# First weights between the input halves, value fills after the second gate, stick-breaking scores inside attention, and an output projection begun on two tiles

## The reference

```python
h = rms_norm(x, norm1_w[l])
cols = split_cols(h @ w_in[l], IN_SIZES)
y_a = short_conv_mixer(a_b, a_c, a_u, conv_w[l], conv_b[l])
y_b = nsa_mixer(...)          # 4 heads: compressed, selected and windowed attention
y_c = mla_mixer(...)          # 4 heads, causal
y_d = stick_breaking_mixer(...)   # 4 heads
y = rms_norm(concat(y_a, y_b, y_c, y_d) in 4 groups of 256)
x = x + y @ w_out[l]
x = x + square(relu(rms_norm(x) @ ffn_w1[l])) @ ffn_w2[l]
```

```python
z = einsum('bqhd,bkhd->bhqk', q_blk, k) * scale
log_1m = where(strict, log_sigmoid(-z), 0.0)
rem = cumsum(log_1m, reverse=True) - log_1m
a = where(strict, exp(log_sigmoid(z) + rem), 0.0)
```

## Time and profile before

| what | value |
| --- | --- |
| time, median of 3 runs | 1802.92 us (1802.78 to 1804.18) |
| the profiled execution's own time | 1803.52 us |
| its span in the trace | 1801.4 us |
| PE busy | 1737.8 us (96% of the span), 8107 matmuls |
| DVE, ACT, POOL busy | 969.2, 692.2, 203.3 us (54%, 38%, 11%) |
| share of the chain that ended last | PE 89%, DVE 5%, ACT 2%, issue 2%, DMA 1% |

### The profile page before, as it was taken

One profiled execution on the slowest core, in us unless ns is written; L12 is line 12 of the kernel. 1 busy time (PEld: TensorE's weight loads), 2 busy tenths in 40 slices (PEclk: granted clock), 3 DMA queues, 4 the chain that ended last, 5 costly groups with the idle time before them and its releaser, 6 DMA issues.

```text
span 1801.4 us, 20984 instructions
## 1 busy us (share of the span) xinstructions
PE 1737.8 (96%) x8107; PEld 1376.0 (76%) x8107; DVE 969.2 (54%) x1724; ACT 692.2 (38%) x1243; POOL 203.3 (11%) x167
## 2 busy tenths in 40 slices
PE   7999999999999999999999899999999999999998
PEld 4557778566888888887788787775887888888887
DVE  4465476343563333346655788875444555556334
ACT  3233344552433233234464545552424422223234
POOL 3233100002100000012000233320200200000000
PEclk9999999899999999999999999999999999999999
DMA  6243201213433323233122011113330223332221
GB/s 186 80 132 95 94 24 48 76 59 99 126 94 94 102 94 108 95 94 98 55 70 71 12 59 59 48 59 99 123 106 1 94 94 97 106 101 94 94 94 47
DMA packets 122371, 152.23 MB, mean 85 GB/s; under 512 B 8827, under 2 KB 110609, under 8 KB 121762
## 3 DMA queue, kind: packets, MB, share of 16 engines
q1 hardware_dynamic: 119986, 140.19, 24.5%
q0 software_dynamic: 2288, 10.71, 1.7%
HBM read 144.90 MB, written 6.00 MB: 84 GB/s over the span
## 4 chain that ended last, share of the span: by engine, by line
PE 89%; DVE 5%; ACT 2%; issue 2%; DMA 1%; POOL 0%; DVEq 0%; ACTq 0%; POOLq 0%
PE bank L1953 50%; PE bank L1987 16%; PE bank L1261 2%; PE bank L1654 2%; PE bank L2198 2%; PE bank L2309 2%; PE bank L1212 1%; PE bank L2282 1%; PE bank L2195 1%; PE bank L774 1%; PE bank L1124 1%; PE bank L1129 1%; PE bank L1351 1%; PE bank L1687 1%; PE bank L2084 1%
## 5 line engine op out<-in xcount | busy, mean ns | idle before, releaser
L1953 PE MATMUL bank<-act_high,w_high 128*128 128x512 f32 x1360 | 553.0, 407 | 13.2 <-issue 4.6
L1953 PE MATMUL bank<-act_high,w_low 128*128 128x512 f32 x1360 | 533.1, 392 | 0.0
L1953 PE MATMUL bank<-act_low,w_high 128*128 128x512 f32 x1360 | 532.3, 391 | 0.0
L643 ACT ACTIVATE w_high<-ring 128x1024 fp32r<-128x1024 f32 x222 | 234.4, 1057 | 680.9 <-PE bank L1953 466.9
L667 DVE TENSOR_TENSOR w_low<-ring,w_high 128x1024 fp32r<-128x1024 f32 x202 | 254.7, 1262 | 221.9 <-ACT w_high L643 221.9
L1953 PEld LDWEIGHTS bank<-act_high,w_high 128*128 128x128 f32 x1360 | 257.6, 189 | 75.0 <-issue 16.8
L1953 PEld LDWEIGHTS bank<-act_high,w_low 128*128 128x128 f32 x1360 | 256.7, 189 | 55.2
L1953 PEld LDWEIGHTS bank<-act_low,w_high 128*128 128x128 f32 x1360 | 257.8, 190 | 51.8 <-issue 3.6
L1987 PE MATMUL bank<-act_high,w_high 128*128 128x512 f32 x416 | 162.2, 390 | 2.4 <-DVE arena L3192 1.2
L1987 PE MATMUL bank<-act_high,w_low 128*128 128x512 f32 x416 | 162.0, 389 | 0.0
L1987 PE MATMUL bank<-act_low,w_high 128*128 128x512 f32 x416 | 162.0, 389 | 0.0
(11 more groups left out here) (361 smaller groups left out, 2187.8 us busy)
## 6 DMA issues: line engine op xcount, KB each, us to landing
ring<-in_ffn_w SPq DMA_DIRECT2D x32, 1024.0 KB, 5.3
ring<-in_w_in SPq DMA_DIRECT2D x28, 1024.0 KB, 5.4
ring<-in_w_up SPq DMA_DIRECT2D x22, 1024.0 KB, 5.1
ring<-in_w_down SPq DMA_DIRECT2D x11, 1024.0 KB, 5.0
ring<-in_w_mem_kv SPq DMA_DIRECT2D x8, 1024.0 KB, 5.4
ring<-in_cmp_w SPq DMA_DIRECT2D x4, 1024.0 KB, 7.9
ring<-in_w_out SPq DMA_DIRECT2D x4, 1024.0 KB, 5.5
ring<-in_w_mix_out SPq DMA_DIRECT2D x4, 1024.0 KB, 5.3
```

What stands on the lines that cost most here:

```text
L643: nc.scalar.activation(part(w_high, name), raw_part(name), ACT.Copy).then_inc(w_rounded, 1)
L1953: last = nc.tensor.matmul(b[0:rows, :], w[:, k, 0:rows], a, start=k == 0 and n == 0, stop=k == KT - 1 and n == 2)
```

## The change

1. **Start.** SP fetches m_q between the halves of x. ACT rounds cq0 after two squares, and cq1 after two act_high. POOL splits both before it waits for x_in[1]. PE runs pieces of cq0 and cq1 between the turns and square sums of the second half. cq0 and cq1 get banks 4 and 5, all later tiles shift in their turn of banks.
2. **Value fills.** The three memsets go from DVE's work at 101 to 106 us to behind its second gate of the short convolution (`conv_gate(1)`, 166 us before).
3. **Stick-breaking scores.** PE makes the four scores of head 0 in units 58 to 61, in banks 2 and 4, ACT their logs in units 60 to 63. The memory key pairs move to units 13 to 54. The wait for `head_out` moves behind the scores of head 1, and the first memory value tile waits until the scores of head 0 have been copied.
4. **Output projection.** After wo0's six steps and the sums for y3, PE runs six steps of wo1, then the last two steps of wo0 and of wo1, then wo2 to wo7.

The diff, without the pure renaming in `stick_logs` (to `stick_log`, one score at a time):

```diff
-        plan("cq0", "dve")
+        plan("cq0", "dve", in_bank=4)
         plan_bias(0, "strip")
-        plan("cq1", "dve")
+        plan("cq1", "dve", in_bank=5)
...
+        def stick_bank(n):
+            return bank[(2, 4)[n % 2] if n < TT else n % 2]
...
-        MEM_KEY_AT = [13 + 8 * i // 5 for i in range(32)]
+        MEM_KEY_AT = [13 + 43 * i // 32 for i in range(32)]
+        STICK_AT = 58
...
+            fetch_input(0)
+            eng.wait_ge(cols_zero, 1)
+            dst, src = gain_load
+            eng.dma_start(dst, src).then_inc(gain_in, 16)
+            fetch(0)
+            fetch_input(1)
+            eng.dma_start(rel_sb[0:32, :], A["rel_bias"]).then_inc(rel_in, 16)
+            for i in range(1, len(loads)):
...
             link(eng, "pool", nc.gpsimd.memset(cmp_bias[64:P, :], 0.0))
+            split_weights(eng, "cq1")
             eng.wait_ge(x_in[1], 16)
...
-            features("cq0", big="in1")
+            features("cq0", big="in1", ks=(0, 1))
+            square_sum(eng, 2)
+            square_sum(eng, 3)
+            for k in range(4, 8):
+                turn_input(k)
+            features("cq0", big="in1", ks=(2, 3))
+            square_sum(eng, 4)
+            features("cq1", 108, ks=range(4))
+            square_sum(eng, 5)
+            features("cq0", big="in1", ks=range(4, 8))
             square_sum(eng, 6)
             square_sum(eng, 7)
             bias_tables(0, "strip")
-            features("cq1", 108)
+            features("cq1", 108, ks=range(4, 8))
...
                     open_tile(eng, name)
+                    if u == 32:
+                        eng.wait_ge(sb_zs, TT)
...
+                if STICK_AT <= u < STICK_AT + TT:
+                    if u < STICK_AT + 2:
+                        taken(eng, f"memk{6 + u - STICK_AT}")
+                    stick_score(eng, 0, u - STICK_AT)
 
             attend_pe(eng, 0, N_B1, ahead_by=2, between=mem_key_pair)
-            eng.wait_ge(head_out, 4)
-            stick_scores(eng, 0)
             for h in range(4):
...
+                if h == 0:
+                    eng.wait_ge(head_out, 4)
...
             norm_sums(eng, "y3")
-            features("wo0", parts="y", ks=(6, 7))
-            for m in range(1, 8):
+            features("wo1", parts="y", ks=range(6))
+            for m in range(2):
+                features(f"wo{m}", parts="y", ks=(6, 7))
+            for m in range(2, 8):
...
+            for k in range(2):
+                taken(eng, f"x{k}")
+                big_square(eng, "in1", k)
+            round_weights(eng, "cq0")
+            eng.wait_ge(cols_out, 1)
             for k in range(4):
                 taken(eng, f"x{k}")
+                gained_high(eng, "in1", k)
+                if k == 1:
+                    round_weights(eng, "cq1")
+            for k in range(2, 4):
                 big_square(eng, "in1", k)
...
+                if STICK_AT + 2 <= u < STICK_AT + 2 + TT:
+                    stick_log(eng, 0, u - STICK_AT - 2)
...
-            nc.vector.memset(nv[:, :, 0:5:2, :], 0.0)
-            nc.vector.memset(vc, 0.0)
...
             conv_gate(1)
+            nc.vector.memset(nv[:, :, 0:5:2, :], 0.0)
+            nc.vector.memset(mv[:, :, 1, :], 0.0)
+            nc.vector.memset(vc, 0.0)
```

More of the change, by code:

```diff
@@ L1343, in stick, with stick_score @@
             return arena[:, at:at + ST_W[kt]]
[L1345 to L1354, removed]
+        def stick_bank(n):
+            return bank[(2, 4)[n % 2] if n < TT else n % 2]
+        def stick_score(eng, h, kt):
+            n = 4 * h + kt
+            if n >= 2:
+                eng.wait_ge(sb_zs, n - 1)
+            r = head_rows(h)
+            nc.tensor.matmul(stick_bank(n)[:, 0:ST_W[kt]], ar(SKT + h // 2)[r, kt * P:(kt + 1) * P],
+                             ar(SQT + h // 2)[r, kt * P:S], start=True, stop=True).then_inc(sb_z, 1)
         def stick_sums(eng, h, between):
@@ L1378, in stick_values, with stick_log @@
             last.then_inc(sb_o, 1)
[L1380 to L1392, removed]
+        def stick_log(eng, h, kt):
+            n = 4 * h + kt
+            eng.wait_ge(sb_z, n + 1)
+            if h >= 2:
+                eng.wait_ge(sb_o, h - 1)
+            z, s = stick(h, kt, 0), stick(h, kt, 1)
+            nc.scalar.activation(z, stick_bank(n)[:, 0:ST_W[kt]], ACT.Copy).then_inc(sb_zs, 1)
+            eng.wait_ge(sb_zs, n + 1)
+            link(eng, "act", nc.scalar.activation(s, z, ACT.Abs))
+            link(eng, "act", nc.scalar.activation(s, s, ACT.Exp, scale=-1.0))
+            nc.scalar.activation(s, s, ACT.Ln, bias=one_col).then_inc(sb_l, 1)
         def stick_softplus(eng, h):
@@ L1808, in _, with fetch_input @@
         def _(eng):
-            for half in range(2):
+            def fetch_input(half):
                 ds = slice(half * S, (half + 1) * S)
                 eng.dma_start(x_tok[:, :, ds], A["x"][0].rearrange("(t p) d -> p t d", p=P)[:, :, ds]).then_inc(x_in[half], 16)
[L1812 to L1816, removed]
             def fetch(i):
@@ L1928, in _ @@
             nc.tensor.transpose(bank[7][0:P, 0:KT], row_stage[0:KT, 0, :], ident[0:KT, 0:KT]).then_inc(cols_turned, 1)
[L1929 to L1934, removed]
             def features(name, rows=P, big=None, parts=None, ks=range(KT)):
@@ L2211, in mem_key_pair @@
                     mem_pair(eng, MEM_KEY_AT.index(u))
+                if STICK_AT <= u < STICK_AT + TT:
+                    if u < STICK_AT + 2:
+                        taken(eng, f"memk{6 + u - STICK_AT}")
+                    stick_score(eng, 0, u - STICK_AT)
             attend_pe(eng, 0, N_B1, ahead_by=2, between=mem_key_pair)
-            eng.wait_ge(head_out, 4)
-            stick_scores(eng, 0)
             for h in range(4):
                 if h + 1 < 4:
-                    stick_scores(eng, h + 1, lambda eng, kt: mem_pair(eng, 32 + 8 * h + kt))
+                    for kt in range(TT):
+                        stick_score(eng, h + 1, kt)
+                        mem_pair(eng, 32 + 8 * h + kt)
+                if h == 0:
+                    eng.wait_ge(head_out, 4)
                 if h in (1, 2):
@@ L2474, in take_mem_k @@
                     take(f"memk{m}", mem_k1[:, 256 * m:256 * (m + 1)], w=256)
+                if STICK_AT + 2 <= u < STICK_AT + 2 + TT:
+                    stick_log(eng, 0, u - STICK_AT - 2)
             attend_act(eng, 0, N_B1, pair_end_b1, take_mem_k)
             take_mem_k(eng, N_B1)
-            stick_logs(eng, 0)
             for h in range(4):
                 if h + 1 < 4:
-                    stick_logs(eng, h + 1)
+                    for kt in range(TT):
+                        stick_log(eng, h + 1, kt)
                 if h in (1, 2):
```

9 lines of the change are left out of this document (1 added, 8 removed).

## The result

The changed kernel takes 1785.84 us (median of 5: 1784.52, 1785.16, 1785.84, 1790.06, 1793.22) against 1802.96 (median of 5: 1802.78 to 1808.2): a ratio of 0.9909, with a 95% interval from 0.9884 to 0.9934. That is 17.1 us faster by the medians, 16.4 by the ratio, where 12.5 were forecast. The range, 1784 to 1800, holds it. A repeat on another occasion gave 1785.82 (1785.28 to 1787.1) and a ratio of 0.9894 [0.9879, 0.9909].

A forecast was written before the change was run, and what follows sets the result against it. PE's waits and lower-clock stretches were taken to bound the kernel. Gains of 1.0 + 0 + 6.9 + 4.6 = 12.5 us off 1803.5 give 1791.0; the median lies 0.6 below, so 1790.4, range 1784 to 1800.

The forecast's parts named there:

- What bounds the kernel: Whole kernel: PE is 89% of the chain, so only its waits, lower clock or cheaper PE work can shorten it.
- The start: First projection: PE begins earlier but is held up by DVE waiting; cq1 ends at 38.7, gain 1.0 us.
- in this time DVE wants to make act_low 0 and 1: First projection: POOL's splits last from 12.1 to 16.9, DVE stands; act_low 0 there at 15.1, act_low 1 at 17.5.
- the start isn't held up: First projection: DVE makes act_low 0 and 1 before POOL starts; gain 4 more, 1786.4 us; chance 0.08.
- the low clock and small waits: First projection: a stretch at 1.2 GHz after PE has stood some 3 us, plus small waits, 4.1 us.
- The value fills: Moved memsets on DVE: they delayed nothing PE waited for; gain 0, bounded by 2.1 us.
- Stick-breaking: Attention's end: 13.3 us off behind it, 0.7 for the sums, attention 7.1 longer; net gain 6.9 us.
- The new waits in the last units: Attention units 60 to 63: ACT's logs and queued exponentials come through to PE, 4.7 us.
- Output projection: Behind y3's sums: wo1 matmuls fill the 4.26 us wait, the clock stays up; gain 4.6 us.
- the clock that stays down: Behind attention: head 1's stretch takes 13.5 us again, attention part gives 0; gain 5.6, 1797.3 us; chance 0.26.
- the slower case: Behind attention: clock stays low and doesn't rise with the suffix sums either, 16.4 us more; 1813.7 us; chance 0.07.
- next to nothing: Clock stays down, start loses 1 us, wo2's wait takes 1.5 more; gain 2.1, 1800.8 us; chance 0.09.

The follow-up runs named there:

- back-to-back kernel: The changed kernel with ACT rounding cq1 right behind cq0, so POOL's two splits run without a gap: 1788.91 us.
- the last four kernels: The changed kernel with gains turned first (1784.98 us), that plus first splits on DVE (1782.90), head-0 scores spread (1790.41), all three edits (1787.60).

## Why the prediction was right, point by point

**What bounds the kernel**: right. In the traces the change gained where PE had stood or run at 1.2 GHz.

**The start**: the term that was mis-sized, 1.0 forecast, 5.6 measured for the part alone. Its mechanism, DVE standing until POOL's split ends, is shown by the back-to-back kernel, by the first profiled execution, where cq1 ended at 39.09 (38.7 forecast), and by the kernels with the splits on DVE, where every act_low takes 0.75 us. The lock of the Trainium skill (SBUF — State Buffer, SBUF: two separate sides) agrees with the row: act_low 0 began at 12.96, the split ended at 11.77 + 2.35 = 14.12, and act_low 0 was done about 0.55 later. The failing step was "in this time DVE wants to make act_low 0 and 1": I set the splits back to back, 12.1 to 16.9, from the earlier trace rows, while ACT's order puts act_high 0 and 1 between its two roundings, so POOL has a gap of up to 1.5 us, and with late gains both act_low fit in. That is the outcome of the rival "the start isn't held up", which I gave 0.08, in the profiled executions of the start alone and of the repeat, but not its mechanism: the two act_low came between the splits, not before the first, and the gain was 3.7 and 3.3 us instead of the rival's 5.0. The other 1.5 us, the clock at 68 us, were in no term. That 39.09 came so near to 38.7 is in part luck. The four records of 1.73 us in the earlier trace rows are two sums, not four: a sum of squares takes 0.86 us, not 0.43. The six square sums are 5.2 us instead of 2.6, and 1.7 of what stands between the tiles are sums counted already, not 0.9. The sum should have read 40.5; the low clock and small waits, put at 4.1, made up for it with about 2.7.

**The value fills**: 0 forecast; the trace shows 0, the times leave 0.2 to 3.4 us open.

**Stick-breaking**: 6.9 forecast, 8.1 measured alone, and by the repeat's trace the sum of terms is almost exact. Attention from the last input tile (196.21 before, 189.71 in the repeat) to its end took 129.7 us and takes 136.7, 7.0 longer (7.1 forecast); behind it 20.5 became 7.2. But terms inside are wrong and cancel, so the near hit on the whole is luck. The new waits in the last units are 2.1 us (2.2 against 0.1), not 4.7, and 1.7 us of waits are there with the key pairs moved and no score or log in these units, so scores and logs together add only about half a microsecond to them. The early key pairs gave 0.5 us back instead of 1.7. The low clock came, about 1.7 us instead of 1.2, but at 200 us and not in the last units. With the scores' own 2.9 these make 6.2; the other 0.8 PE counts as busy, the kernel with the key pairs alone shows 0.7 of them, and where they come from stays open.

**Output projection**: 4.6 forecast, 4.1 in the trace, 4.5 alone. The new wait for wo2 is 1.2 us (1.1 forecast), and wo2 begins 10.2 us after the start of the sums for y3 instead of 9.8, by longer hand-overs.

**The rivals**: the clock that stays down didn't come: it was 1.00 from 320 to 348 us in both executions of the changed kernel. So neither did the slower case, nor "next to nothing".

## What to carry to other kernels

Where PE waits for another engine and its clock falls behind, price the wait with the low stretch that follows: here 3.7 us of waits at the stick-breaking scores (3.0, and 0.7 for the last attention output) were followed by a stretch at 1.2 GHz that cost about 7.0 more (13.5 - 7.2 of head 1, and 0.7 of the sums). Work that fills such a wait saves both: at the output projection 18 matmuls of the next tile filled 4.3 us and saved 1.7 us of low clock behind it, of which about 1.8 us were lost again, most of it in the new wait for wo2. A step of DVE with two SBUF inputs shouldn't be left to race a POOL split: the order that puts the split on DVE, at half the time (1.23 us against 2.35), and the turn of the gains first ended the first projection earliest here (35.33 us), and had the lowest median. Work that covers waits should not be taken from where it covers them: the key pairs gave 0.5 us where they went and left 1.7 us of waits where they had been. And a profile of one execution can be several microseconds from the median: read a second before explaining a small difference.

## What the runs showed of the hardware

Executions of one kernel differ in where PE runs slowly. Between 9.5 and 12.5 us the weight loads of the square sums took 0.19 us in some executions and 0.34 in others, at a granted clock that reads 1.00 in both; the gains' turn then came at 11.66 or 12.94, and this decided the contest above. Where ACT's roundings stand as in the change and POOL splits, the turn came at 10.40, 11.66 and 11.79 us in three profiles, and cq1 ended at 37.98, 39.09 and 37.58; in two it came at 12.60 and 12.94, and cq1 ended at 36.09 and 36.47. So in the repeat a slower PE made the start faster. Weight loads before the turn of the gains, in the first profiled execution and in the repeat:

```profile
10.71 0.19 PEld L887 LDWEIGHTS bank<-sq,const_sb 128*128 128x128 f32 x1 [0.24 <-issue]
```
```profile
11.80 0.34 PEld L887 LDWEIGHTS bank<-sq,const_sb 128*128 128x128 f32 x1 [0.52 <-issue]
```

The wait of about 1 us that ends between 63 and 70 us is in all profiles. It was followed by a low clock in all five with the old start (before, the stick-breaking part, the output projection, the key pairs and the fills alone) and in two of nine with the new one. What decides it stays open. So does what made the clock fall at 1140 to 1143 us in the profiles of three of the last four kernels.
